# One weight unit in full fp32: items of one block multiply the eighth unit as it lies in memory, with four fp32 products in place of twelve rounded ones

## What is computed

```python
logits = h @ router_w + router_b                # 32 experts, each token takes 4
top_logit, top_idx = lax.top_k(logits, TOP_K)
...
def expert_block(args):                         # one block of tokens of one expert
    tok, g, e = args
    xb = h_pad[tok]
    gu = xb @ w_gate_up[e] + b_gate_up[e]       # 1024 -> 2048
    gate, up = jnp.split(gu, 2, axis=-1)
    gate = jnp.minimum(gate, 7.0)
    up = jnp.clip(up, -7.0, 7.0)
    act = (up + 1.0) * (gate * jax.nn.sigmoid(1.702 * gate))
    y = act @ w_down[e] + b_down[e]             # 1024 -> 1024
    return y * g[:, None]
```

## Time and profile before

| | |
|---|---|
| profiled execution, its own time | 2243.18 us |
| its span, first to last instruction | 2241.5 us |
| median of the runs | 2239.04 us |
| granted TensorE clock, mean | 0.978 of full speed |
| TensorE matmul busy | 2138.9 us (95%) |
| TensorE weight load busy | 1778.7 us (79%) |
| VectorE busy | 1559.4 us (70%) |
| ScalarE busy | 1331.0 us (59%) |
| GpSimd busy | 348.9 us (16%) |
| share of the chain that ended last | PE 83%, issue 7%, DVE 5%, ACT 3% |

### The profile page before, as it was taken

One profiled execution on the slowest core, in us unless ns is written; L12 is line 12 of the kernel. 1 busy time (PEld: TensorE's weight loads), 2 busy tenths in 40 slices (PEclk: granted clock), 3 DMA queues, 4 the chain that ended last, 5 costly groups with the idle time before them and its releaser, 6 DMA issues.

```text
span 2241.5 us, 33895 instructions
## 1 busy us (share of the span) xinstructions
PE 2138.9 (95%) x10706; PEld 1778.7 (79%) x10707; DVE 1559.4 (70%) x1646; ACT 1331.0 (59%) x1521; POOL 348.9 (16%) x306
## 2 busy tenths in 40 slices
PE   6999999895999999999999999999999999999995
PEld 5889767895778888878887878788888878888884
DVE  4321289566577578788768888886776888677756
ACT  5111179444465467677557777775655777565745
POOL 1000000023111022122112112221111322111201
PEclk9999999997899999999999999999999999999998
DMA  5121300534787689799869999996667999767955
GB/s 201 57 91 41 113 1 2 187 106 126 263 295 246 199 280 359 234 377 369 291 214 379 372 369 360 373 344 229 226 228 233 349 375 343 229 222 243 322 177 187
DMA packets 265845, 538.68 MB, mean 240 GB/s; under 512 B 14581, under 2 KB 31247, under 8 KB 265696
## 3 DMA queue, kind: packets, MB, share of 16 engines
q1 hardware_dynamic: 248848, 490.35, 61.5%
q0 software_dynamic: 16944, 47.63, 8.6%
HBM read 501.65 MB, written 38.59 MB: 241 GB/s over the span
## 4 chain that ended last, share of the span: by engine, by line
PE 83%; issue 7%; DVE 5%; ACT 3%; DMA 1%; POOL 0%; ACTq 0%; SPq 0%; DVEq 0%; POOLq 0%
PE ps L734 79%; ACT hT_hi L1191 1%; PE ps L956 1%; PE ps L963 1%; DVE hT_lo L1648 1%; DVE w_lo L1637 1%; PE ps L866 1%; ACT region_mem L1226 0%; DVE work L1688 0%; DVE hT_lo L1658 0%; DMA weight_ring<-in_w_mix_in 0%; ACT hT_lo L1239 0%; DVE work L1461 0%; POOL expert_lists L608 0%; PE ps L921 0%
## 5 line engine op out<-in xcount | busy, mean ns | idle before, releaser
L734 PE MATMUL ps<-hT_hi,hT_lo 128*128 128x512 f32 (+1 forms) x4256 | 1384.7, 388 | 12.7 <-DVE hT_lo L1658 12.3
L734 PEld LDWEIGHTS ps<-hT_hi,hT_lo 128*128 128x128 f32 x4256 | 797.7, 188 | 181.2 <-DVE w_lo L1637 18.1
L1191 ACT ACTIVATE hT_hi<-weight_ring 128x2048 fp32r<-128x2048 f32 x417 | 785.9, 1913 | 163.0 <-PE ps L734 102.8
L1637 DVE TENSOR_TENSOR slots_between<-weight_ring,hT_hi 128x2048 fp32r<-128x2048 f32 x245 | 552.4, 2287 | 122.4 <-ACT hT_hi L1191 121.9
L734 PE MATMUL ps<-slots_between,hT_lo 128*128 128x512 f32 x1344 | 525.7, 391 | 0.0
L1637 DVE TENSOR_TENSOR w_lo<-weight_ring,hT_hi 128x2048 fp32r<-128x2048 f32 x140 | 319.7, 2284 | 33.9 <-ACT hT_hi L1191 33.9
L734 PE MATMUL ps<-w_lo,hT_lo 128*128 128x512 f32 (+1 forms) x896 | 336.2, 375 | 0.0
L734 PEld LDWEIGHTS ps<-slots_between,hT_lo 128*128 128x128 f32 x1344 | 253.2, 188 | 53.8
L734 PEld LDWEIGHTS ps<-w_lo,hT_lo 128*128 128x128 f32 x896 | 168.7, 188 | 30.5
L628 POOL DMA_INDIRECT residual_rows<-work,idx_now x47 | 113.5, 2415 | 384.5 <-ACT work L1252 237.6
L622 POOL DMA_INDIRECT work<-normed_rows,idx_far x49 | 75.8, 1547 | 550.3 <-PE ps L956 449.1
(11 more groups left out here) (259 smaller groups left out, 2448.6 us busy)
## 6 DMA issues: line engine op xcount, KB each, us to landing
weight_ring<-in_w_gate_up SPq DMA_DIRECT2D x280, 1024.0 KB, 8.0
weight_ring<-in_w_down SPq DMA_DIRECT2D x140, 1024.0 KB, 6.4
weight_ring<-in_w_mix_in SPq DMA_DIRECT2D x10, 1024.0 KB, 6.7
weight_ring<-in_x SPq DMA_DIRECT2D x8, 512.0 KB, 8.3
weight_ring<-in_w_mix_out SPq DMA_DIRECT2D x4, 1024.0 KB, 5.3
work<-in_x SPq DMA_DIRECT2D x8, 512.0 KB, 5.7
residual_rows<-work SPq DMA_DIRECT2D x8, 512.0 KB, 2.8
normed_rows<-work SPq DMA_DIRECT2D x8, 512.0 KB, 3.6
```

The costliest lines, as they stand in the source:

```text
L734: return pe.matmul(o, l, r, start=first, stop=last)
L1191: act.activation(w_high_part(u), ring[:, home(u), :], ACT.Copy).then_inc(s["w_high_made"], 1)
L1637: dve.tensor_tensor(w_low_part(u), ring[:, home(u), :], w_high_part(u).bitcast(f32), ALU.subtract)\
```

## The change

In items of one block, unit 7 is neither copied by ScalarE nor subtracted by VectorE. TensorE waits for its arrival in the ring and multiplies it there, as fp32, with unrounded tokens: four products instead of twelve. The unrounded tokens of row groups 4 to 7 (the second row half, the one that unit 7 covers) are copied by ScalarE from PSUM bank 7 to a free place in a region of SBUF (`x_plain`, in `region_v`), by `keep_plain`, at the place in the order where before stood the bare count for "no second block"; the copy waits until VectorE has read the same bank. The counts on the high and low semaphores that unit 7 gave are given by unit 8 together with its own. Items of two blocks take unit 7 as before.

```diff
+        def unit_slot_of(u):
+            return ring[:, home(u), :].rearrange("p (k n) -> p k n", k=4)
...
+        PLAIN = 7
+        x_plain = r_v[:, :].rearrange("p (k b s t) -> p k b s t", k=KD, b=BLOCKS, s=2)[:, 4:8, 1, 0, :]
...
                 rows = a_split if side == "d" else x_split
+                if len(kinds) == 1 and u == PLAIN:
+                    pe.wait_ge(s_w[home(u)], arrived(u, it))
+                    pe.wait_ge(s_xhigh[1], it + 1)
+                    for kk in range(4):
+                        last = mm(ps[:, out_bank(side, c, 0, kinds), :], x_plain[:, kk, :], unit_slot_of(u)[:, kk, :], False, kk == 3)
+                    last.then_inc(s["w_used"], 1)
+                    return
                 pe.wait_ge(s["w_low_made"], it * 12 + (u + 1))
...
-            def high_unit(it, u):
+            def high_unit(it, u, count=1):
...
-                act.activation(w_high_part(u), ring[:, home(u), :], ACT.Copy).then_inc(s["w_high_made"], 1)
+                act.activation(w_high_part(u), ring[:, home(u), :], ACT.Copy).then_inc(s["w_high_made"], count)
+
+            def keep_plain(it):
+                act.wait_ge(s_xlow[0], it + 1)
+                act.activation(x_plain, ps[:, 7, :].rearrange("p (k t) -> p k t", t=P), ACT.Copy).then_inc(s_xhigh[1], 1)
...
                 up_rest(it, 0, kinds)
-                high_unit(it, 7)
+                if len(kinds) > 1:
+                    high_unit(it, 7)
                 gate_rest(it, 1, kinds)
                 sigmoids(it, 1, kinds)
                 a_high(it, 0, kinds)
-                high_unit(it, 8)
+                high_unit(it, 8, 2 if len(kinds) == 1 else 1)
...
-                    by_second(act, size_next, lambda kind: x_high(1, it + 1, kind), lambda: act.sem_inc(s_xhigh[1], 1))
+                    by_second(act, size_next, lambda kind: x_high(1, it + 1, kind), lambda: keep_plain(it + 1))
...
-            by_second(act, size_first, lambda kind: x_high(1, 0, kind, 2), lambda: act.sem_inc(s_xhigh[1], 1))
+            by_second(act, size_first, lambda kind: x_high(1, 0, kind, 2), lambda: keep_plain(0))
...
                 low_unit(it, 6)
-                low_unit(it, 7)
+                if len(kinds) > 1:
+                    low_unit(it, 7)
                 gates(it, 1, kinds)
                 a_low(it, 0, kinds)
-                low_unit(it, 8)
+                low_unit(it, 8, 2 if len(kinds) == 1 else 1)
```

More of the change, by code:

```diff
@@ L220, in hymba_kernel @@
         a_split = split[:, 4096:8192].rearrange("p (k b s t) -> p k b s t", k=KD, b=BLOCKS, s=2)
+        PLAIN = 7
+        assert UNITS[PLAIN][0] != "d" and UNITS[PLAIN][2] == 1
+        x_plain = r_v[:, :].rearrange("p (k b s t) -> p k b s t", k=KD, b=BLOCKS, s=2)[:, 4:8, 1, 0, :]
         ident = sb("ident", [P, P])
@@ L1631, in _, with low_unit @@
             dve.wait_ge(s["tab_made"], 1)
-            def low_unit(it, u):
+            def low_unit(it, u, count=1):
                 dve.wait_ge(s["w_high_made"], it * 12 + (u + 1))
                 dve.tensor_tensor(w_low_part(u), ring[:, home(u), :], w_high_part(u).bitcast(f32), ALU.subtract)\
-                    .then_inc(s["w_low_made"], 1)
+                    .then_inc(s["w_low_made"], count)
             def low_place(part, kind):
```

## The result

The changed kernel takes 2246.58 us (median of 11 runs, 2243.96 to 2249.20), the kernel before, run beside it, 2240.19 us (11 runs, 2238.82 to 2242.16). The ratio is 1.0028, 95% interval 1.0018 to 1.0037: slower by 6.4 us (4.0 to 8.3). The forecast was +5.5, and 2244.5 against the earlier median of 2239.04; the range was 2240.5 to 2251.5.

The account below looks back on a forecast made before the run. TensorE was taken as the bound, waiting at unit 10 for VectorE's chain; fifteen items 3.0, six items 2.3 and the last 0.2 made +5.5 us, 2244.5 against the median of 2239.04, range 2240.5 to 2251.5.

Parts of the forecast that it names:

- Bound and chain: TensorE bounds; the chain from unit 5's end through high 8, low 8 and a_low(1) to unit 10 excludes high 7, low 7.
- Items: Of 22 one-block items, 15 show the wait at unit 10, 6 precede a two-block item, one is last.
- Step 1: Unit 7 on TensorE: eight fp32 records take 3.43 us against 2.73 for twelve rounded products, +0.70 us.
- rival A: At each unit 7, changing product kind costs 0.29 us more, so 0.99: +11.9 us, 2250.9; chance 0.13.
- C: Unit 7's fp32 products go at half rate, 1.72 us; no item changes, 2239.0 us; chance 0.07.
- Step 2: VectorE's clamp waits for the longer unit 7: 0.50 us of cushion used up, the chain 0.20 us later.
- Step 3: Fifteen one-block items: a_low(1) decides unit 10's start, 0.20 us each, 3.0 us; printed wait falls to about 0.4.
- Step 4: Six items followed by two blocks: TensorE arrives 0.60 later at unit 10, 0.21 absorbed, 0.39 each, 2.3 us.
- Step 5: Last item 0.2 us; two-block items keep their code; the keep_plain copy's cover on ScalarE is just used up, 0.
- Sum: Whole kernel: 3.0 + 2.3 + 0.2 = +5.5 us, 2244.5 against the median of 2239.04.
- D: Faster: the freed 4.2 us an item let the chain to unit 10 begin earlier and shorten its wait; chance 0.04.

Follow-up runs that it names:

- e1: Changed kernel with ScalarE's high part and VectorE's subtraction for unit 7 put back, result unread, TensorE waiting for it: 2245.92 us, 1.0024 times the kernel before.
- e3: Changed kernel with five fp32 products for unit 7 instead of four: 2264.62 us, 1.0110 times the kernel before.
- e4: Changed kernel with high 8 and low 8 early and low 9 before products(1) in one-block items: 2233.62 us, 0.9967 times the kernel before.
- e6: Changed kernel with high 8 and low 8 early in one-block items, low 9 left in place: 2246.08 us, 1.0023 times the kernel before.
- e7: Kernel before, unit 7 still split, with high 8 and low 8 early in one-block items, low 9 left in place: 2230.30 us, ratio 0.9954.
- e2: Changed kernel with three fp32 products for unit 7 instead of four: 2242.38 us, 1.0006 times the kernel before.

## Why the prediction was right

- **Bound and chain.** Right. High 7 and low 7 were not on it: putting them back (e1) changes nothing.
- **Items.** 15, 6 and 1, as the item-by-item differences show.
- **Step 1, +0.70 us.** Right: 3.43 us measured, four fp32 products of 0.858 each, in eight records. Three and five products give 2.57 and 4.29. Neither the 0.29 us of rival A nor the half rate of C appears. By that row the factor of two that the Trainium skill ("Perfetto Trace Analysis", Engine Utilization) lists for FP32_LOW_HIGH doesn't price such a product, and its four passes ("FP8 and Floating Point Precision", TensorE Precision Notes) agree with this trace: 0.858 us for 512 columns at 2.4 GHz, whose single pass is 0.213. Two details of the working were off, without effect: 14.0 less 0.16 over 64 is 0.2163 and not 0.2157 (a unit of 3.44), and A's row was not the only one with 512 columns, since the attention part has 96 unsplit records of 64x512. The trace of before could also have weakened A more than I let it: its group of 128x256 starts 0.23 us after the last rounded product (252.76 to 252.99), the usual distance.
- **Step 2, the clamp.** Right: 0.20 us after the next TensorE start in the changed kernel, in e3, e4 and e6. The cushion of 0.50 is shown twice: the line through e3 and the changed kernel puts it at 0.48 to 0.53, and e7 turns it into a gain of 0.51. That e2 gains nothing over the kernel before shows only that VectorE's chain decides there, since its unit 7 is shorter than the rounded one.
- **Step 3, fifteen items.** 0.22 each instead of 0.20, 3.3 us instead of 3.0. The printed wait fell to 0.50, not 0.4: TensorE came 0.52 later, not 0.60, since the hidden wait at unit 9 was 0.14 and not 0.1, and another 0.05 went in first products that no longer followed a wait. It changed nothing, because the chain decides there.
- **Step 4, six items.** The weakest term: 0.27 each instead of 0.39, 1.6 us instead of 2.3. TensorE's arrival decides there, as said: in all six the first product of unit 10 starts 14.61 us after `turn_a(0)` before and 14.97 in the changed kernel, 0.36 later, and right behind the transposes (0.79 instead of 0.96 to 1.00). The working had left out what follows: 0.09 of the 0.36 are got back by the end of the next item's first unit. What gives them back I didn't pursue.
- **Step 5.** +0.25 for the last item (0.2); the copy is hidden, as said, with 0.36 us to spare where I had it just used up.
- **Sum.** +5.3 in two pairs of traces, +5.0 and +6.4 in two sets of runs, against +5.5. That it comes so near is in part luck: the fifteen items gave 0.3 us more than forecast, the two-block items and the last 0.2, and the six 0.7 less. Both ratios, 1.0028 and 1.0022, lie beyond the 0.2% line, but both intervals reach below it (1.0018 and 1.0012): that the kernel is slower is shown, that it is slower by 0.2% is not. This is the closeness that 0.61 for slower and 0.35 for the same allowed for.
- **D.** The argument held for this order of the work. It would have been worth saying that the clamp itself is a bound only for what stands behind it: e4 takes `low 9` from behind it and is faster than the kernel before, though the kernel before gains more by the same.

## What to carry to other kernels

Work taken from an engine with idle time is a gain only if it stands in the chain of what the bound engine waits for; draw that chain backwards from the wait before counting its microseconds. A step made longer beside such a chain is priced by its cushion: measure how long after its end the instruction that needs it really starts, and compare with one that is known to wait. And the order of the work alone was worth 24 us, where the printed waits of the busiest engine at that place came to 12.3 us (15 times 0.8): waits that the view doesn't print went with them. The exchange of arithmetic moved 5 to 16.6 us in the orders tried here.

## What the runs showed of the hardware

- Unsplit fp32 with 128x512 moving data: two records a product, 0.429 us each, so 0.858, where a rounded product takes 0.2275. On TensorE alone three rounded ones (0.68 us) are cheaper than one unrounded, by 0.18 us.
- Changing between rounded and unrounded products cost nothing measurable: 0.23 us from the last rounded start (1255.04) to the first fp32 one (1255.27), and 0.43 from the last fp32 record to the transposes. Six, eight and ten records take 2.57, 3.43 and 4.29 us, 0.43 for each and no fixed part beside them.
- VectorE starts 0.19 to 0.20 us after the next TensorE start where it waits for a product's end, the same after a rounded unit (e7) and after an fp32 one (the changed kernel, e3, e4, e6).
- The experts' part, which follows some 20 us in which TensorE did little and was granted 0.50, runs its first matmuls at half clock for a stretch that differs from run to run (granted clock 0.50 to 0.79 over the same 8 us), which moved item 0 by more than 1 us.
